# Mixture-of-experts stage: experts in 32 token places, four side by side in column quarters of the array, unrounded, weights in 8 KB runs

## The chip, the cores and the metric

One core of a Trainium2 chip runs the whole program. The metric is the device time of one execution in microseconds; the kernel before takes 2503.92 us, median of 3 runs (2502.22 to 2505.46).

## What is computed

The program is two blocks one behind the other on 256 tokens of width 1024, all in float32. The first has two layers of feed-forward, four kinds of attention and feed-forward again; the second has a gated delta rule, an RWKV-7 scan, their merge and a mixture of experts. Only the last concerns the change. Cut to it, the reference is:

```python
def hier_moe(h, router_grp, router_grp_b, router_exp, router_exp_b, w_gate, w_up, w_down):
    t = h.reshape(-1, h.shape[-1])                       # 256 tokens x 1024
    grp_p = softmax(t @ router_grp + router_grp_b)       # 4 groups
    p_grp, g_sel = lax.top_k(grp_p, 1)                   # one group to a token
    exp_logits = (t @ router_exp + router_exp_b).reshape(-1, 4, 8)
    in_grp = take_along_axis(exp_logits, g_sel)          # 8 experts of that group
    top_logit, top_idx = lax.top_k(in_grp, 2)            # two experts to a token
    w_top = softmax(top_logit) * p_grp
    combine = one_hot(group) * one_hot(expert) * w_top   # 256 x 4 x 8
    for grp in range(4):                                 # expert: 1024 -> 2 x 256 -> 1024
        hid = silu(t @ w_gate[grp]) * (t @ w_up[grp])
        out = out + (hid * combine[:, grp]) @ w_down[grp]

# in second_block, at its end
h_lat = h_lat + m_lat[2] * y_lat
h_lat = h_lat + m_lat[5] * hier_moe(modulate(rmsnorm(h_lat, norm_ffn_g), m_lat[3], m_lat[4]), ...)
return rmsnorm(h_lat, final_norm_g)
```

There are 32 experts, each with three matrices of 1 MB (gate and up 1024 x 256, down 256 x 1024), 100.7 MB in all.

## The kernel before

Everything is written out by hand for five engines, with semaphores that `did` and `at` number by name. Activations stand with the model's width on the partitions (`XT`, 8 tiles of 128 x 256 tokens).

**Weights.** All weights come over one queue, SP's, in the order of the list `jobs`. `load_ring` (L408, its DMA is L416) puts job j into slot j mod 3 of the ring `RB` (3 slots of 2 MB) as soon as the job three before it has been used up. `fill_e` (L334) fills a slot with an expert's gate and up matrices; a partition gets eight rows of each, every one a run of 1 KB. `fill_d` (L341) takes the down matrices of two experts, in runs of 4 KB.

**Products.** `mm` (L283, the matmul itself is L284) is one product. A float32 product leaves two records in the trace. `mm3` and, in the experts, the same thing written out, does a product in three rounded ones: ACT rounds half a slot into `gwh` (`Stream.high`, L440), DVE takes the rest into `gwl` (`Stream.low`, L449), activations are split likewise (`gxh`, `gxl`, `ghh`, `ghl`), and PE multiplies high by low, low by high and high by high. A slot is free when DVE has done its second half (`("low", "g", n)`).

**Around the experts.** `merge` (L3062) ends the second block's mixers: PE does four gate tiles (`gate1_pe`), the small product `glo`, turns, eight `merge` tiles and eight `out2` tiles, and between the `out2` tiles `Route.pe` does the router's products and turns the tokens. `places_dve` (L3362) then finds each token's group (`sel`, marked `grouped`), its place in the group by a product with a triangle (`ranks` in `places_pe`, L3320) and a 0/1 matrix `CHOSEN` of 128 tokens x 4 groups x 128 places. Then `known` says whether every group has at most 128 tokens; if so `gathered` (L3489) runs, else `dense` (L3622), over all tokens. `places_pe` gathers the tokens of all four groups at once by products with `CHOSEN` (`xm`), ACT scales them (L3352) and rounds them (L3355), DVE takes the rest (L3374).

**The experts.** `gathered` goes through 32 experts: 24 products of 128 places by 512 columns for gate and up, silu on ACT (L3571), times the token's weight on DVE (L3595), two turns (L3529), rounding, and 12 products of 512 columns down into the group's sums. Per group the sums are kept (L3582, L3609), and at the end products with the turned `CHOSEN` spread them over the tokens, and the last norm and its turns (`Finish`, L3749) run between them, up to the four stores (L3809).

Of the kernel before, what the change touches and what calls it, by code (L numbers as in the profile page):

```python
# [38 lines left out]
def constants():  # L39
# [21 lines left out]
    for k in range(6):  # L61
# [13 lines left out]
    pe_once="lam cum ab ab_parts route ranks cw glo wide_c spread shifted", eg="dg", ed="dd", columns="merge mgate out2 conv shift z",  # L75
    rw_in="w_in ic_in cums bon_in k_in", gdn_in="re_gate cumg wide_g kk kb_t",
    act_once="lam_exp sine f_log g_log beta group_exp expert_exp spread_root lnx_root o_root sil w2 low_act xd_high",
# [4 lines left out]
             "renorm_sq lnx_square a2 logits group_in expert_in combined rank known chosen cw_out cb_t xd_low rt_bias rt_w rstd_x grouped",  # L82
# [141 lines left out]
def program(nc, A, out, known):  # L224
    stack = ExitStack()
    with stack:
# [74 lines left out]
        jobs, job_no = [], {}  # L301

        def job(key, fill, free):
            job_no[key] = len(jobs)
            jobs.append((fill, free))
# [89 lines left out]
        pairs = [(("e", 0), ("e", 1))]  # L395
        pairs += [(("e", e), ("e", e + 1), ("d", e - 2)) for e in range(2, 32, 2)] + [(("d", 30),)]
        PAIRS = [x for step in pairs for x in step]
        first_expert = len(jobs)

        def slot_of(*key):  # L400
            return RB[:, job_no[key] % NSLOT, :]

        def landed(*key):
            return at(f"ring{job_no[key] % NSLOT}", job_no[key])

        sent = [0]

        def load_ring(upto_job):  # L408
            while sent[0] < upto_job:
                j = sent[0]  # L410
                if j >= NSLOT:
                    SP.wait_ge(*at(*jobs[j - NSLOT][1]))
                for i, (dst, src) in enumerate(jobs[j][0](RB[:, j % NSLOT, :])):
                    if i and one_by_one_from <= j < one_by_one_to:
                        SP.wait_ge(*at(f"ring{j % NSLOT}", j, i - 1))
                    nc.sync.dma_start(dst, src).then_inc(*did(f"ring{j % NSLOT}", j, i, by=16))  # L416
                did(f"ring{j % NSLOT}", j, by=0)
# [3468 lines left out]
```

## Time and profile before

| what | us |
|---|---|
| median of 3 runs | 2503.92 |
| span of the profiled execution | 2506.8 |
| PE busy in it | 2421.1 |
| DVE busy | 1408.6 |
| ACT busy | 1193.3 |

The profiled execution is 2.9 us above the median. Times below are counted from its start. The page's second part cuts the span into 40 slices of 62.7 us; the expert stage lies in the last five. PE is busy to 97% over the span, DMA moves 158 GB/s in the mean and over 360 GB/s in three of the last slices, so the mean hides that stage.

### The profile page before, as it was taken

What the parts mean: (1) busy time and instruction counts of PE and PEld (TensorE: products, weight loads), DVE (VectorE), ACT (ScalarE), POOL (GpSimd) and SP (SyncE); (2) the same over time, 40 slices, a digit from 0 to 9 for tenths busy, and PEclk for the clock granted to TensorE, in tenths of its full rate; (3) what the DMA queues carried; (4) which work ended last, traced back from release to release, by engine and by line L of the source; (5) the groups of instructions that cost most, each with busy time, mean ns of one, the idle gap of its engine ahead of it and who ended that gap; (6) DMA issues with size and microseconds to landing.
All of it is one profiled execution on the core that took longest, in us unless ns stands there. A gap on an engine that the chain in (4) does not pass through costs nothing.

```text
span 2506.8 us, 52399 instructions
## 1 busy us (share of the span) xinstructions
PE 2421.1 (97%) x23215; PEld 2091.8 (83%) x23215; DVE 1408.6 (56%) x2208; ACT 1193.3 (48%) x1725; POOL 296.2 (12%) x417
## 2 busy tenths in 40 slices
PE   7999999999999999999999999899999888999998
PEld 7999888799999998878899995686477777878887
DVE  5655544366646655543666567454434454378886
ACT  5434465444344444474454346431255342277775
POOL 0100000031101100000301000462133222000000
PEclk9999999999999999999999999999999989999999
DMA  8754522266656755422457522201201111479995
GB/s 262 243 205 152 205 92 92 105 202 216 223 183 202 236 185 179 146 97 106 143 193 236 213 77 101 70 3 40 68 35 37 33 42 46 131 246 365 368 364 181
DMA packets 269445, 396.15 MB, mean 158 GB/s; under 512 B 9624, under 2 KB 173133, under 8 KB 269085
## 3 DMA queue, kind: packets, MB, share of 16 engines
q1 hardware_dynamic: 267481, 389.32, 45.6%
q8 instruction: 185, 3.03, 0.5%
q0 software_dynamic: 1120, 2.17, 0.3%
q10 hardware_dynamic: 612, 1.24, 0.1%
q14 instruction: 47, 0.39, 0.0%
HBM read 391.66 MB, written 1.05 MB: 157 GB/s over the span
## 4 chain that ended last, share of the span: by engine, by line
PE 82%; DVE 6%; DMA 5%; ACT 3%; issue 2%; SPq 1%; POOL 0%; ACTq 0%; DVEq 0%
PE ps L284 81%; DMA RB<-in_moe_w_up 5%; DVE gwl L449 2%; ACT gwh L440 1%; SPq L521 1%; PE ps L1151 0%; SPq L416 0%; DVE wl L449 0%; DVE AR L659 0%; ACT wh L440 0%; ACT AR L2903 0%; DVE AR L1972 0%; PE ps L543 0%; ACT AR L2895 0%; ACT AT L1205 0%
## 5 line engine op out<-in xcount | busy, mean ns | idle before, releaser
L449 DVE TENSOR_TENSOR wl<-RB,wh 128x2048 fp32r<-128x2048 f32 (+5 forms) x189 | 412.2, 2185 | 281.1 <-ACT wh L440 280.6
L284 PE MATMUL ps<-H,RB 128*128 128x256 f32 (+2 forms) x1728 | 451.7, 420 | 2.8 <-ACT AR L2874 1.3
L440 ACT ACTIVATE wh<-RB 128x2048 fp32r<-128x2048 f32 (+5 forms) x189 | 342.2, 1814 | 227.4 <-PE ps L284 200.0
L284 PEld LDWEIGHTS ps<-H,RB 128*128 128x128 f32 (+1 forms) x1728 | 320.2, 189 | 113.7 <-issue 75.6
L284 PE MATMUL ps<-xhf,wl 128*128 128x256 f32 x1408 | 402.4, 286 | 2.4 <-DVE xlf L688 2.4
L284 PE MATMUL ps<-xlf,wh 128*128 128x256 f32 x1408 | 398.9, 283 | 0.0
L284 PE MATMUL ps<-xhf,wh 128*128 128x256 f32 x1408 | 398.8, 283 | 0.0
L284 PE MATMUL ps<-AR 64*64 64x64 f32 (+3 forms) x8296 | 264.6, 236 | 39.9 <-issue 24.7
L284 PEld LDWEIGHTS ps<-AR 64*64 64x64 f32 (+2 forms) x8296 | 231.4, 142 | 79.1 <-issue 64.2
L284 PEld LDWEIGHTS ps<-xhf,wl 128*128 128x128 f32 x1408 | 270.6, 192 | 13.2 <-issue 9.4
L284 PEld LDWEIGHTS ps<-xlf,wh 128*128 128x128 f32 x1408 | 270.8, 192 | 0.1
L284 PEld LDWEIGHTS ps<-xhf,wh 128*128 128x128 f32 x1408 | 270.6, 192 | 0.0
L449 DVE TENSOR_TENSOR gwl<-RB,gwh 128x2048 fp32r<-128x2048 f32 x96 | 217.2, 2289 | 37.2 <-ACT gwh L440 35.8
L440 ACT ACTIVATE gwh<-RB 128x2048 fp32r<-128x2048 f32 x96 | 183.0, 1925 | 44.1 <-DMA RB<-in_moe_w_up 30.8
L284 PE MATMUL ps<-hh,wl 128*128 128x256 f32 x704 | 199.2, 283 | 0.0
L284 PE MATMUL ps<-hl,wh 128*128 128x256 f32 x704 | 199.2, 283 | 0.0
L284 PE MATMUL ps<-hh,wh 128*128 128x256 f32 x704 | 199.2, 283 | 0.0
L793 ACT ACTIVATE H<-H 128x256 f32<-128x256 f32 x88 | 36.8, 419 | 296.0 <-DVE H L829 296.0
L284 PEld LDWEIGHTS ps<-hh,wl 128*128 128x128 f32 x704 | 135.2, 192 | 0.0
L284 PEld LDWEIGHTS ps<-hl,wh 128*128 128x128 f32 x704 | 135.2, 192 | 0.0
L284 PEld LDWEIGHTS ps<-hh,wh 128*128 128x128 f32 x704 | 135.2, 192 | 0.0
L1472 POOL TENSOR_TENSOR H<-H 128x256 f32<-128x256 f32 x48 | 47.6, 1026 | 680.5 <-DVE H L1443 680.3
(445 smaller groups left out, 4108.1 us busy)
## 6 DMA issues: line engine op xcount, KB each, us to landing
RB<-in_ffn_w_gu SPq DMA_DIRECT2D x88, 1024.0 KB, 7.7
RB<-in_w_in SPq DMA_DIRECT2D x23, 2048.0 KB, 7.8
RB<-in_ffn_w_down SPq DMA_DIRECT2D x16, 2048.0 KB, 7.8
RB<-in_w_gate SPq DMA_DIRECT2D x16, 2048.0 KB, 8.9
RB<-in_moe_w_gate SPq DMA_DIRECT2D x32, 1024.0 KB, 7.6
RB<-in_moe_w_up SPq DMA_DIRECT2D x32, 1024.0 KB, 10.2
RB<-in_moe_w_down SPq DMA_DIRECT2D x32, 1024.0 KB, 8.2
RB<-in_ada_w SPq DMA_DIRECT2D x12, 2048.0 KB, 9.9
```

Source lines behind the costliest of these rows:

```text
L284: return M.matmul(o, lhsT, rhs, start=start, stop=stop, skip_group_check=True)
L440: S.activation(self.pair(h)[0], of(slot_of(*key)), ACT.Copy).then_inc(*did("high", *mark))
L449: V.tensor_tensor(lo, of(slot_of(*key)), hi.bitcast(F32), ALU.subtract).then_inc(*did("low", *mark))
L521: nc.sync.dma_start(dst, src).then_inc(*did("late", by=16))
L793: S.activation(sil[:, n % 4, 0, :], sil[:, n % 4, 0, :], ACT.Silu).then_inc(*did("silu", f, n))
L1472: P.tensor_tensor(HB[:, c, :], HB[:, c, :], tmp[:, (8 * i + c) % 4, :], ALU.add).then_inc(*did("merged", l, br, c))
```

## The change

- **Loads.** `moe_jobs` lists, for each of eight steps of four experts, four gate-and-up jobs and two down jobs of two experts. Both fills give a partition one contiguous run of 8 KB per MB: row p·8+k of a matrix goes to partition p for gate and up, row p·2+h for down. Beside the three ring slots there are six more (`EX0` to `EX5`), in memory that the splits and the scan's buffers had; each opens at a mark in `opened`. Nine expert jobs are queued before the router has decided, and the second `out2` load comes behind the first three.
- **Order of the width.** Since a partition now holds rows p·8+k, tokens are gathered in that order (`UT` written strided), and the scale and shift vectors are brought into it once (`OWN`: five small DVE instructions and 8 + 1 small products in `merge`, one more copy, one product and a sum on DVE).
- **Places.** A rank is counted for each of 32 experts instead of each of 4 groups; `chosen` makes 32 places for each expert. The experts of a token must be known before the ranks, so that chain on DVE comes first. `known` asks for at most 32 tokens per expert. If an expert has more, `dense` runs, which is unrounded too.
- **Products.** Nothing is split or rounded. One step multiplies four experts, each by its own 32 places: stationary 128 x 32, moving 128 x 512, output in 32 of the 128 PSUM partitions. Per step these are 16 products for `gather`, 32 for `up`, 16 for `down` and 4 for `spread`, which adds straight into four banks of sums by token. `rows_pe` puts the residual into these banks first, `Y` is multiplied by the last gate as it leaves PSUM, and the last norm works on rows, without turns.

```diff
         def fill_e(e):
             def f(slot):
-                v = slot.rearrange("p (k g n) -> p k g n", k=KD, g=2)
-                return [(v[:, :, s, :], rows(A[n][0, e // 8, e % 8]))
+                v = slot.rearrange("p (s n) -> p s n", s=2)
+                return [(v[:, s, :], A[n][0, e // 8, e % 8].rearrange("(p k) n -> p (k n)", k=KD))
                         for s, n in ((0, "moe_w_gate_2"), (1, "moe_w_up_2"))]
             return f
 
-        def fill_d(e):
+        def fill_d(n, x):
             def f(slot):
-                v = slot.rearrange("p (e k n) -> p e k n", e=2, k=2)
-                return [(v[:, u], rows(A["moe_w_down_2"][0, e // 8, e % 8 + u])) for u in range(2)]
+                e = 4 * (n % 2) + 2 * x
+                return [(slot.rearrange("p (e n) -> p e n", e=2), A["moe_w_down_2"][0, n // 2, e:e + 2].rearrange(
+                    "e (p h) n -> p e (h n)", h=2))]
             return f
...
+        out2_last = jobs.pop()
+
+        slots = [RB[:, i, :] for i in range(NSLOT)] + [sb(f"EX{i}", STAGE + c, [4096]) for i, c in enumerate(
+            (13568, 17664, 21760, 9472, 4736))] + [sb("EX5", O_H, [4096])]
+        opened = {3: [("rw_out", 7, 1)], 4: [("rw_out", 7, 1)], 5: [("rw_out", 7, 1)], 6: [("turned", "ya", 1)],
+                  7: [("summed", 7)], 8: [("mgate", 1, 7), ("glo", 1)]}
+        expert_slots = (3, 4, 5, 8, 6, ring_jobs[0] % NSLOT, (ring_jobs[0] + 1) % NSLOT, (ring_jobs[0] + 2) % NSLOT, 7)
 
...
+        sent, holder = [0], {}
 
         def load_ring(upto_job):
             while sent[0] < upto_job:
                 j = sent[0]
-                if j >= NSLOT:
-                    SP.wait_ge(*at(*jobs[j - NSLOT][1]))
-                for i, (dst, src) in enumerate(jobs[j][0](RB[:, j % NSLOT, :])):
+                fill, free, slot = jobs[j]
+                if slot in holder:
+                    SP.wait_ge(*at(*jobs[holder[slot]][1]))
+                else:
+                    for mark in opened.get(slot, ()):
+                        SP.wait_ge(*at(*mark))
+                holder[slot] = j
+                for i, (dst, src) in enumerate(fill(slots[slot])):
...
+                PE.wait_ge(*at("own_in"))
+                ps = bank(("own_rows",), ("own_16",))
+                for k in range(KD):
+                    ins = mm(ps[0:16, 16 * k:16 * k + 16], ident.rearrange("p (q k) -> p k q", k=KD)[:, k, :], OWN_IN,
+                             True, True)
+                ins.then_inc(*did("own_rows"))
...
+                ps = bank(("own",), ("own_out",))
+                PE.wait_ge(*at("own_16"))
+                mm(ps[:, 0:128], RST[0:16, 128:256], RST[0:16, 0:128], True, True).then_inc(*did("own"))
...
+                V.tensor_copy(OWN_IN[:, 0:8], SCL[:, 2, :])
+                V.tensor_copy(OWN_IN[:, 8:16], MOD[:, 24:32, 0])
+                V.tensor_copy(RST[0:16, 128:256].rearrange("p (c q) -> p c q", c=8),
+                              ident[0:16, 0:16].unsqueeze(1).broadcast_to([16, 8, 16]))
+                V.tensor_reduce(IN_16, ident.rearrange("p (c j) -> p c j", c=8), AXX, ALU.add)
+                V.tensor_reduce(IN_32, ident.rearrange("p (c j) -> p c j", c=4), AXX, ALU.add).then_inc(*did("own_in"))
...
+            ring_jobs[0] = ring_at_experts
+            of_experts = [(kind, n, x) for n in range(8) for kind, x in
+                          (("e", 0), ("e", 1), ("e", 2), ("e", 3), ("d", 0), ("d", 1))]
+            for i, (kind, n, x) in enumerate(of_experts):
+                if i == 3:
+                    job_no[("out2", 1)] = len(jobs)
+                    jobs.append(out2_last)
+                slot = expert_slots[i % len(expert_slots)]
                 if kind == "e":
+                    job(("e", 4 * n + x), fill_e(4 * n + x), ("eg", n) if branch == "g" else ("dg", 4 * n + x), slot)
                 else:
+                    job(("d", n, x), fill_d(n, x),
+                        ("dd", n, x) if branch == "d" else ("y", n, 1), slot)
...
-                self.ws_g = Split("g", Stream(self.wh, self.wl), halves)
...
+            def rows_pe(self):
+
+                for c in (0, 4):
+                    for t in LAT:
+                        ps = bank(("acc", t, c // 4), among=(4, 5, 6, 7))
+                        for j in range(4):
+                            ins = mm(ps[:, 128 * j:128 * j + 128], XT[:, c + j, 128 * t:128 * t + 128], ident, j == 0,
+                                     False)
+                ins.then_inc(*did("acc"))
...
+                one = self.px.rearrange("p t g e -> p t (g e)")
+                PE.wait_ge(*at("picked"))
+                mm(ps[:, 64:96], ones, one[:, 0], True, False)
+                mm(ps[:, 64:96], ones, one[:, 1], False, True)
+                mm(ps[:, 0:32], cst(C_PAIR), one[:, 0], True, True)
+                mm(ps[:, 32:64], ones, one[:, 0], True, False)
+                mm(ps[:, 32:64], cst(C_PAIR), one[:, 1], False, True).then_inc(*did("ranks"))
...
+                def chosen(t, n0, n1):
+                    e = 4 * (n1 - n0)
+                    return V.tensor_tensor(
+                        self.CHOSEN[:, t, n0:n1].rearrange("p n (e s) -> p (n e) s", e=4),
+                        CST[:, C_NUM + 1:C_NUM + 33].unsqueeze(1).broadcast_to([128, e, 32]),
+                        rank[:, t, 4 * n0:4 * n1].unsqueeze(2).broadcast_to([128, e, 32]), ALU.is_equal)
...
+                def gather(n):
+                    for t in LAT:
+                        PE.wait_ge(*at("chosen", t, min(n, 2)))
+                    for half in range(2):
+                        ps = bank(("xm", n, half), ("xm_out", n, 4 * half + 3), among=work)
+                        for k in range(4 * half, 4 * half + 4):
+                            for t in LAT:
+                                if n == 0 and k == 0:
+                                    PE.wait_ge(*at("u_rows", t, 4))
+                                ins = mm(ps[:, 128 * (k % 4):128 * (k % 4) + 128], UT[:, t, k, :], CHOSEN[:, t, n], t == 0,
+                                         t == 1)
+                        ins.then_inc(*did("xm", n, half))
+
+                def up(n):
+                    ps = bank(("up", n), ("h_scaled", n), among=work)
+                    for k in range(KD):
+                        PE.wait_ge(*at("xm_out", n, k))
+                        for c in range(4):
+                            PE.wait_ge(*landed("e", 4 * n + c))
+                            ins = mm(ps[32 * c:32 * c + 32, :].rearrange("p (s n) -> p s n", s=2),
+                                     XG[n % 2][:, k, 32 * c:32 * c + 32], up_of(4 * n + c)[:, :, k, :], k == 0, k == KD - 1)
+                    ins.then_inc(*did("eg", n))
+
+                def back(n):
+                    turn(("turned", "back", n), [("back", n)], [CHOSEN[:, t, n] for t in LAT], among=work)
+
+                def turned(n):
+                    PE.wait_ge(*at("h_scaled", n))
+                    turn(("turned", "h", n), [("h_out", n)], [S1[n % 2].rearrange("p (q h) -> p h q", h=2)[:, h, :] for h in range(2)], among=work)
+
+                def down(n):
+                    ps = [bank(("y", n, o), ("y_out", n, o), among=work) for o in range(2)]
+                    PE.wait_ge(*at("h_out", n))
+                    for x in range(2):
+                        PE.wait_ge(*landed("d", n, x))
+                    w = [slot_of("d", n, x).rearrange("p (e h n) -> p e h n", e=2, h=2) for x in range(2)]
+                    for o in range(2):
+                        for half in range(2):
+                            for c in range(4):
+                                ins = mm(ps[o][32 * c:32 * c + 32, :], HT[n % 2][:, half, 32 * c:32 * c + 32],
+                                         w[c // 2][:, c % 2, half, 512 * o:512 * o + 512], half == 0, half == 1)
+                        ins.then_inc(*did("y", n, o))
+
+                def spread(n):
+                    PE.wait_ge(*at("back", n))
+                    for t in LAT:
+                        for o in range(2):
+                            PE.wait_ge(*at("y_out", n, o))
+                            ins = mm(accs[2 * t + o], BACK[n % 2][:, 128 * t:128 * t + 128], Y[:, 512 * o:512 * o + 512],
+                                     False, n == 7)
+                            if n == 7:
+                                ins.then_inc(*did("moe_sum", t, o))
+                    if n < 7:
+                        ins.then_inc(*did("spread", n))
...
-                        ps = bank(("up", "g", e), ("h_scaled", e), among=work)
-                        for half in range(2):
-                            hi, lo = ws.weights(ups[e] + half)
-                            for i in range(4):
-                                k = 4 * half + i
-                                PE.wait_ge(*at("xm_low", k))
-                                a, c = xh[:, k, 128 * g:128 * g + 128], xl[:, k, 128 * g:128 * g + 128]
-                                mm(ps[:, :], c, hi[:, i, :], k == 0, False)
-                                mm(ps[:, :], a, lo[:, i, :], False, False)
-                                ins = mm(ps[:, :], a, hi[:, i, :], False, k == KD - 1)
-                            ins.then_inc(*did("eg", e, half))
-                    elif what == "turn":
-                        ps = bank(("turned", "h", e), ("h_low", e), among=work)
...
+                for n in range(8):
+                    if n:
+                        up(n)
+                        if n < 7:
+                            gather(n + 1)
+                    back(n)
+                    turned(n)
+                    down(n)
+                    spread(n)
...
+                def places(n):
+                    for k in range(KD):
+                        AC.wait_ge(*at("xm", n, k // 4))
+                        if n > 1 and k == 0:
+                            AC.wait_ge(*at("eg", n - 2))
+                        S.activation(XG[n % 2][:, k, :], ps_of("xm", n, k // 4)[:, 128 * (k % 4):128 * (k % 4) + 128],
+                                     ACT.Identity, bias=PV[:, k, 1:2], scale=PV[:, k, 0:1]).then_inc(*did("xm_out", n, k))
...
+                for t in LAT:
+                    for o in range(2):
+                        AC.wait_ge(*at("moe_sum", t, o))
+                        S.activation(SQ[o], accs[2 * t + o], ACT.Square, accum_out=SS[:, t, o:o + 1]).then_inc(
+                            *did("squared", "end", t, o))
+                    AC.wait_ge(*at("sums", t))
+                    S.activation(SS[:, t, 2:3], SS[:, t, 2:3], ACT.Sqrt, bias=EPS[:, 0:1], scale=1.0 / DM).then_inc(
+                        *did("root", "end", t))
+                AC.wait_ge(*at("rstd", "end", 1))
...
+                for n in range(8):
+                    DV.wait_ge(*at("h_silu", n))
+                    V.scalar_tensor_tensor(out=S1[n % 2], in0=S1[n % 2], scalar=CW[:, n:n + 1], in1=ps_of("up", n)[:, 256:512],
+                                           op0=ALU.mult, op1=ALU.mult).then_inc(*did("h_scaled", n))
+                    DV.wait_ge(*at("turned", "h", n))
+                    if n > 1:
+                        DV.wait_ge(*at("y", n - 2, 1))
+                    V.tensor_copy(HT[n % 2].rearrange("p a n -> p (a n)"), ps_of("turned", "h", n)[:, 0:T]).then_inc(
+                        *did("h_out", n))
+                    for o in range(2):
+                        DV.wait_ge(*at("y", n, o))
+                        DV.wait_ge(*at("m5", o))
+                        if n:
+                            DV.wait_ge(*at("spread", n - 1))
+                        V.tensor_tensor(Y[:, 512 * o:512 * o + 512], ps_of("y", n, o), M5[:, 512 * o:512 * o + 512],
+                                        ALU.mult).then_inc(*did("y_out", n, o))
```

## Rows read from the trace of the kernel before

**Rows 1.** The page: span, then DMA share (tenths) and GB/s in 40 slices.
```profile
span 2506.8 us, 52399 instructions
...
DMA  8754522266656755422457522201201111479995
GB/s 262 243 205 152 205 92 92 105 202 216 223 183 202 236 185 179 146 97 106 143 193 236 213 77 101 70 3 40 68 35 37 33 42 46 131 246 365 368 364 181
```

**Rows 2.** Stretches (start:end, length, busy us and count by engine, clock, DMA share, GB/s).
```profile
2148.00:2184.40 36.40, 36.35 (x208) 32.62 (x206) 9.16 (x13) 6.94 (x11) 0.00 (x0) 1.00 0.40 120
2184.40:2190.60 6.20, 2.14 (x11) 2.06 (x11) 3.73 (x24) 4.17 (x7) 0.00 (x0) 0.66 0.94 310
2190.60:2210.00 19.40, 19.40 (x57) 9.83 (x57) 9.78 (x30) 12.43 (x18) 0.00 (x0) 0.84 0.34 109
2210.00:2485.00 275.00, 273.45 (x1224) 222.29 (x1222) 237.50 (x166) 203.46 (x169) 0.00 (x0) 1.00 0.98 336
2485.00:2507.00 22.00, 13.04 (x106) 12.46 (x106) 6.51 (x13) 9.67 (x22) 0.00 (x0) 0.85 0.15 51
```

**Rows 3.** SP: its waits (us, times, longest); its DMA issues in time.
```profile
SPq L416 <- DVE gwl L449: 218.0, 44, 24.8
...
2217.36 0.88 SPq L416 DMA_DIRECT2D RB<-in_moe_w_down  x2
```

**Rows 4.** Groups of instructions 2185 to 2502: busy us, mean ns, idle before.
```profile
L284 PE MATMUL ps<-gwh,gxl 128*128 128x512 f32 x256 | 101.8, 397 | 0.1
L284 PE MATMUL ps<-AR 128*128 128x512 f32 x32 | 17.0, 697 | 2.2 <-DVE SM L3416 2.2
L3529 PE MATMUL ps<-CST,AR 128*128 128x128 f32 x64 | 12.1, 270 | 0.0
L3609 DVE TENSOR_TENSOR gxl<-ps,gxh 128x512 fp32r<-128x512 f32 x8 | 5.1, 683 | 4.5 <-ACT gxh L3582 4.5
```

**Rows 5.** PE in order of time, 2112 to 2169: start, us, instruction, count.
```profile
2112.14 1.97 PE L284 MATMUL ps<-SM 128*128 128x36 f32 x16
...
2127.93 1.95 PE L284 MATMUL ps<-H,AR 128*64 128x256 f32 x16
...
2164.88 3.70 PE L284 MATMUL ps<-AR,RB 128*128 128x256 f32 x16
```

**Rows 6.** Weight loads beside them, 2126 to 2134: ns min/median/max, first and last start.
```profile
L284 PEld LDWEIGHTS ps<-H,AR x16: 132/137/137, 2127.9 to 2129.3; 128*64 128x64 f32 x16
```

**Rows 7.** Stretches: down in runs of 4 KB twice, gate and up of 1 KB.
```profile
2220.00:2224.00 4.00, 4.00 (x21) 3.25 (x20) 4.00 (x5) 2.87 (x4) 0.00 (x0) 1.00 1.03 417
...
2222.00:2223.00 1.00, 1.00 (x6) 0.83 (x5) 1.00 (x2) 1.00 (x1) 0.00 (x0) 1.00 1.05 434
...
2234.00:2236.00 2.00, 2.00 (x10) 1.67 (x9) 1.76 (x4) 1.50 (x2) 0.00 (x0) 1.00 1.10 350
```

**Rows 8.** Stretches: the scan, then two short ones around the router.
```profile
2050.00:2100.00 50.00, 40.89 (x1543) 37.66 (x1543) 24.91 (x61) 17.88 (x43) 19.10 (x32) 0.93 0.04 7
...
2186.00:2188.00 2.00, 1.77 (x9) 1.77 (x10) 0.43 (x3) 1.98 (x4) 0.00 (x0) 0.61 1.07 364
...
2196.00:2198.00 2.00, 2.00 (x6) 0.79 (x5) 0.58 (x1) 0.66 (x1) 0.00 (x0) 0.83 1.10 355
```

**Rows 9.** DVE in order of time: before the merge, and around the router.
```profile
2129.14 1.48 DVE L3170 TENSOR_TENSOR AR<-AR,ps 128x512 f32<-128x512 f32 x2 [2.99 <-PE ps L284]
...
2186.21 0.22 DVE L3399 TENSOR_TENSOR AR<-AR 128x64 f32<-128x64 f32 x1
...
2190.53 0.26 DVE L3417 TENSOR_REDUCE AR<-AR 128x16 f32<-128x64 f32 x1
...
2192.45 0.17 DVE L3438 TENSOR_TENSOR AR<-AR 128x16 f32<-128x16 f32 x1
```

**Rows 10.** The end in order of time: ACT's root, DVE's scaling.
```profile
2499.39 0.26 ACT L3786 ACTIVATE SM<-ps,SM 128x2 f32<-128x2 f32 x1 [0.70 <-PE ps L284]
...
2499.88 1.41 DVE L3801 TENSOR_SCALAR AR<-ps,SM 128x512 f32<-128x512 f32 x2
```

More of the change, by code:

```diff
@@ L74 @@
 SHARED = {name: sem for sem, names in dict(
-    pe_once="lam cum ab ab_parts route ranks cw glo wide_c spread shifted", eg="dg", ed="dd", columns="merge mgate out2 conv shift z",
+    pe_once="lam cum ab ab_parts route ranks cw glo wide_c spread shifted own_rows own acc m5_rows", eg="dg", ed="dd", columns="merge mgate out2 conv shift z",
     rw_in="w_in ic_in cums bon_in k_in", gdn_in="re_gate cumg wide_g kk kb_t",
-    act_once="lam_exp sine f_log g_log beta group_exp expert_exp spread_root lnx_root o_root sil w2 low_act xd_high",
+    act_once="lam_exp sine f_log g_log beta group_exp expert_exp spread_root end_root xd_out lnx_root o_root sil w2 low_act",
     rows="k_rows v_rows rv_rows o_rows u_rows back ob b_rows k_rows_r", h_high="d_high yk_high", h_silu="d_silu",
@@ L298, in everyone, with job @@
                     x.wait_ge(*at(*mark))
-        jobs, job_no = [], {}
-        def job(key, fill, free):
+        jobs, job_no, ring_jobs = [], {}, [0]
+        def job(key, fill, free, slot=None):
             job_no[key] = len(jobs)
-            jobs.append((fill, free))
+            if slot is None:
+                slot = ring_jobs[0] % NSLOT
+                ring_jobs[0] += 1
+            jobs.append((fill, free, slot))
         def fill_gu(w, c):
@@ L3121, in tensor @@
                 route.pe(KD - 1)
+                route.rows_pe()
             def scalar():
@@ L3459, in places_dve @@
                     *did("combined"))
-                for k in range(3, KD):
-                    low_x(k)
-                    if k == 4:
-                        self.ws_g.low(3)
         def experts(route):
@@ L3472, in experts @@
             fits = nc.values_load(route.FLAG[0:1, 0:1], min_val=0, max_val=1)
-            here = ([dict(x.seen) for x in (PE, DV, AC, PO, SP)], dict(counts.n), dict(bank_at), list(bank_free), sent[0])
+            here = ([dict(x.seen) for x in (PE, DV, AC, PO, SP)], dict(counts.n), dict(bank_at), list(bank_free), sent[0],
+                    dict(holder))
             with nc.If(fits > 0):
                 load_ring(len(jobs))
-                gathered(area, route)
+                gathered(route)
             for x, seen in zip((PE, DV, AC, PO, SP), here[0]):
@@ new lines, in scalar @@
+                AC.wait_ge(*at("owned"))
+                for k in range(KD):
+                    AC.wait_ge(*at("xd", k))
+                    S.activation(XM[:, k, :], ps_of("xd", k)[:, 0:T], ACT.Identity, bias=PV[:, k, 1:2],
+                                 scale=PV[:, k, 0:1]).then_inc(*did("xd_out", k))
+                for j, (n, c, i) in enumerate(order):
+                    AC.wait_ge(*at("dg", 4 * n + c))
+                    if j > 1:
+                        AC.wait_ge(*at("c_scaled", *order[j - 2]))
+                    S.activation(S1[:, j % 2, :], ps_of("up", "d", n, c, i)[:, 0:T], ACT.Silu).then_inc(
+                        *did("d_silu", n, c, i))
```

499 lines of the change are left out of this document (185 added, 314 removed).

## The prediction, made before the kernel ran

> **What bounds the kernel now.** I read the page's slices first, then busy time by stretches, then SP's waits, then groups of instructions in the expert stage. Over the whole span DMA moves little, but from slice 36 to 39 it is busy to nine tenths at 365 to 368 GB/s [rows 1]. The change touches only what comes after 2110, so the last 400 us are all that counts. There the stages are [rows 2]: `out2` with the router's products to 2184.4, PE full; the choice of places to 2190.6, PE busy 2.1 of 6.2 us; gathering to 2210, PE full but at a clock of 0.84; the experts to 2485, PE busy 273.5 of 275.0 us; the end, 22 us. PE bounds the expert stage. Its 36 products to an expert start every 0.23 us (1152 products and 64 turns in 275 us). That DMA looks full too is no second bound: SP waited 218.0 us, 44 times, for DVE to free a slot [rows 3], so three slots hold the loads to PE's pace.
>
> **What the change takes away.** All of those 275 us of rounded products, with ACT's and DVE's splits beside them, and the 19.4 us of gathering. What replaces them is bounded by the slower of two streams, PE's and DMA's.
>
> **PE's new price.** An unrounded product of 128 x 256 costs 3.70/8 = 0.46 us with its neighbours' overlap, or 0.43 by the pace of full rows [rows 5]; of 512 columns 0.85 us, two records (the 16 `xm` products left 32 records with a mean of 0.70 us at a mixed clock [rows 4]). If four side by side run at once, `up` costs 8 x 0.85 = 6.8 us a step and `down` 4 x 0.85 = 3.4. Do they? The nearest row is `glo`: eight products of 256 columns with 64 stationary columns, in the two column halves in turn, took 1.95 us in 16 records [rows 5]; one behind the other they would be 8 x 0.43 = 3.4. Two at once is shown at full gain; four at once is not. Bounds: four at once, or two at once (`up` 13.6, `down` 6.8). I take four, since the gain of two was whole.
>
> The Trainium skill ("TensorE: Matmul & The Clock Gate", Part 3, What overlaps and what doesn't) speaks against it: weight loads overlap running products only where the row group differs, and column quarters share all rows. The `glo` weight loads took 137 ns each and their 16 records still came every 107 ns [rows 6]; so the trace doesn't agree with that rule for halves. By it, 96 loads a step would stand bare, about 96 x 0.11 = 10.6 us, which gives 30 us a step instead of 19.
>
> The rest of a step: `gather` 16 products of 128 columns, no cheaper than the 128x36 ones at 1.97/8 = 0.246 [rows 5], so 3.9 us; four turns at 0.135 each, 0.5 (two records of 0.27 overlap [rows 4]); `spread` 4 x 0.85 = 3.4; waits of PE for the copy of the turned tile 0.5 and for the second half of `Y` 0.7, as 128x512 takes DVE 0.68 [rows 4]. `gather` of the next step hides silu and weighting (under 1 us). Sum: 6.8 + 3.4 + 3.9 + 0.5 + 3.4 + 1.2 = 19.2 us a step. ACT (eight scalings, silu, one copy) and DVE (about 2.3 us) lie under it.
>
> **DMA's new price.** A step needs 6 x 2.097 = 12.6 MB. Runs of 1 KB flow at 350 GB/s, runs of 4 KB at 417 over 4 us and 434 in the best single microsecond [rows 7]. No row shows 8 KB. Bounds: 350 (no gain) to 434; I take 417, the nearest run length. That is 30.2 us a step, more than PE's 19.2, so **DMA becomes the bound** and PE idles about 11 us in 30.
>
> Two rules of the Trainium skill differ here ("DMA: Bandwidth & Descriptors"). Where 436 GB/s comes from says that the HBM side, about 358 GB/s to a core, binds; the trace's 417 and 434 disagree. Measured gives 425 for one core with a large transfer, an estimate by which the stream below is 192.5 us instead of 196.1.
>
> **The sum, on the clock of the profiled execution.**
>
> 1. To `route`. On PE `own_rows` (8 narrow products) and `own` come onto the path, 1 to 2.2 us by 0.12 to 0.246 each; I take 1.5. The DVE instructions (about 1 us at first, 0.7 later) are hidden: DVE ends early and waits 2.99 us for `glo` [rows 9]. If the chain were 2 us longer, PE would wait. The early loads go behind the first `out2` load and ahead of the second, which is needed only at 2166; 6.3 MB in front of it are 15 us from 2112. SP passes all its waits in order. Result 2184.4 + 1.5 = 2185.9.
> 2. The places. `grouped` stands as before. The chain from the reduction to the last sum, 2190.5 to 2192.6, now comes before the ranks [rows 9]: +2.2 us. Eight `chosen` comparisons of 1.66 us before become two, about 0.6: -1.1. `rows_pe` (16 products, 3.9 us) runs in PE's idle time. First gather at 2190.6 + 1.5 + 1.1, about 2193.5 with 0.3 of waiting.
> 3. `gather` and `up` of step 0. The clock fell to its lower level of 1.2 GHz in 2186 to 2188, after PE had idled, and rose again in 2196 to 2198 [rows 8], 6 us after work began. I let it do the same: 7.0 us of gathering, then 6.8. End 2207.3. Both at full clock would give 2204, both at half 2214.
> 4. Then slots open again. By now nine of 48 expert jobs are in (the ninth is sent when `out2` ends, 4.2 MB with the eighth, 10 us). Left: 39 x 2.097 = 81.8 MB, at 417 GB/s 196.1 us. End of loads 2403.4. A stall would come if `y` of step 0 were later than 20 us after `up`; I count `cw` 3.9, gather 3.9, `m5_rows` 2.0, turns 0.5, wait 0.5, down 3.4 = 14.2. From there the slack grows.
> 5. Behind the last load: `down` 3.4, `Y` 0.8, `spread` 3.4, and 2.7 because PE has been idle and starts at the low clock; square, root and scaling 2.0; stores 5.5, as from the last scaling's end at 2501.3 to 2506.8 [rows 10]. Together 17.8.
>
> End 2403.4 + 17.8 = 2421.2, that is 85.6 below 2506.8. The profiled execution lies 2.9 above the median, so 2503.9 - 85.6 = **2418.3 us**.
>
> **The rivals.**
>
> - *The transfers gain nothing from longer runs.* For: the mean was 366 over whole slices [rows 1], and no row has 8 KB. Against: 417 at 4 KB. At 366 the stream takes 223.5 us: 2446. At 350 it is 234: 2456.
> - *Only two quarters run at once*, or weight loads stand bare. A step is 19.2 + 6.8 + 3.4 = 29.4 us, about equal to DMA's. The first `up` ends at 2214.1; then 8 steps, 235.2, less one `up` and one `gather`, 17.5, with 6 for `cw` and `m5_rows` and 7.5 behind the last `spread`: 2445.3, as a median 2442.
>
> The page's rule on weight loads gives 30 us a step, 5 more in all.
> - *Slower: the quarters run one behind the other.* `up` 27.3 and `down` 13.7 make a step 50.0 us; eight steps 400, from 2200.5, less one `gather` 3.9, with 6 and 7.5: 2610, as a median 2607, 103 slower. It decides from a step of (2506.8 - 2200.5 - 9.6)/8 = 37.1 us, that is below 1.5 quarters at once. Against it: the halves in `glo`.
> - *No gain: the clock.* DMA-bound PE idles 11 us in each 30, and the clock falls after idling [rows 8]. If it stayed at 1.2 GHz for the whole stage, a step would be 18 x 2 + 1.2 = 37.2, eight 298; from 2200.5, less 7.8 for a `gather`, with 12 and 7.5: 2510, as a median 2507, just about no change, and slower with any other loss. Against it: in the scan PE is idle 9 of 50 us and works in 64x64 tiles, at a clock of 0.93 [rows 8], and a PE that slow would not idle at all. One slow start in each step costs 3 us of the 11 to spare, nothing.
> - *It doesn't do what it says*: an expert with over 32 tokens sends everything down the dense branch, 32 x 16 x 0.85 + 32 x 16 x 0.43 = 655 us, about 2870. The reference's own routing of these inputs gives the fullest expert 27 tokens, so this has almost no chance.
>
> **How the numbers follow.** Forecast (DMA-bound, 400 to 434 GB/s, 2410 to 2430) 0.60; transfers without gain or partly 0.15; two at once or bare loads, and other PE costs that end in 2430 to 2460, 0.15; one behind the other 0.05; the clock 0.04; dense 0.01. The range reaches from 434 GB/s with `up` at full clock (2407) down a little for the end stage, 2403, to the cases at 2445 and 2456: 2455. A measurement of this kernel can tell about 0.2%, 5 us, from no change. Faster 0.89: the first three cases are 0.90, less 0.01 for what no row shows, which goes to no change. Slower 0.08: 0.05, half of the clock's 0.04 and 0.01. Within 0.2% 0.03.
>
> **What would show it.** In the profile after: DMA at 400 or more GB/s from about 2207 to 2403 with a share near 1, PE idle some 10 us in 30 and waiting for `in_moe_w_gate` or `in_moe_w_down`; `up` records every 107 ns at full clock; the first `up` ended by 2207; the last load 18 us before the end. Wrong would be: PE busy without gaps, records every 213 ns, SP waiting for PE, or a lasting clock of 0.5.

## The result and the profile after

The changed kernel takes **2414.74 us**, median of 4 runs (2412.0 to 2415.13), the kernel before 2503.07 beside it (2501.75 to 2505.46): a ratio of 0.9646 (95% interval 0.9632 to 0.966), 88 us less. The forecast was 2418.3. Its profiled execution took 2412.8 us.

The page of the changed kernel, where [rows 1] stood: span and instructions, busy time by engine, then clock, DMA share and GB/s in slices that are now 60.3 us long.

```profile
span 2412.8 us, 51780 instructions
...
PE 2293.6 (95%) x23049; PEld 1925.2 (80%) x23049; DVE 1178.6 (49%) x2070; ACT 1003.7 (42%) x1613; POOL 297.5 (12%) x417
...
PEclk9999999999999999999999999999999999999998
DMA  8754533255655754442346752220111101177997
GB/s 266 244 201 166 175 128 105 88 202 184 213 210 165 255 202 174 165 138 85 110 171 200 241 192 74 105 72 4 41 70 37 39 20 57 34 287 293 420 420 322
```

DVE and ACT are little used in the last slices, and DMA is at 420 GB/s where it was at 366. Executions differ by some us before the stage that was changed: `out2` and the router's products end at 2180.4 here and at 2184.4 before, although this change only adds to what comes ahead of them, and in another execution of the changed kernel (`e10_same` below) they end at 2190.4. I therefore also count every run from the end of the router's last product (the last `128x2` product that `Route.pe` issues) to the end of the span, and call that **the rest**. It was 322.4 us before (2506.8 - 2184.4) and is 232.4 now: 90.0 less.

Stretches of the changed kernel, columns as in [rows 2]: the choice of places; the first `gather`; the first `up`; the stage; behind it. The last two lines show where the loads really stop.

```profile
2180.40:2188.70 8.30, 4.95 (x42) 4.84 (x42) 5.31 (x33) 5.73 (x8) 0.00 (x0) 1.00 1.02 425
2188.70:2192.50 3.80, 3.79 (x36) 3.68 (x37) 2.46 (x9) 1.51 (x4) 0.00 (x0) 1.00 0.67 262
2192.50:2199.50 7.00, 7.00 (x66) 1.97 (x65) 0.00 (x0) 2.79 (x5) 0.00 (x0) 1.00 0.01 3
2199.50:2395.80 196.30, 156.96 (x1030) 67.96 (x1027) 16.41 (x30) 26.67 (x72) 0.00 (x0) 0.91 1.01 416
2395.80:2413.00 17.20, 9.48 (x54) 2.92 (x45) 6.52 (x15) 6.12 (x15) 0.00 (x0) 0.90 0.21 78
...
2396.00:2397.00 1.00, 1.00 (x6) 0.11 (x1) 0.00 (x0) 0.00 (x0) 0.00 (x0) 1.00 0.43 180
2397.00:2398.00 1.00, 0.47 (x3) 0.20 (x2) 0.44 (x1) 0.84 (x3) 0.00 (x0) 1.00 0.00 0
```

The fourth line is the stage: DMA full for 196.3 us, PE at work in 157.0 of them. The loads then thin out: the last packet of a weight ends at 2397.2, and the last load counts as landed at 2397.6. The third line is a gap: all nine slots are full, nothing can be loaded until the first `up` frees four.

One stretch of the chain that ended last, in order of time (start, us, what).

```profile
2336.92 20.89 DMA EX<-in_moe_w_up
...
2357.86 8.97 PE ps L284 x58
...
2366.84 0.33 SPq L429
...
2367.21 20.47 DMA EX<-in_moe_w_up
...
2387.72 9.39 PE ps L284 x58
```

PE's 9 us stand in the chain, although DMA doesn't stop in them. The profile draws it so: `up` frees a slot, SP sends a load into it, and that load lands 20 us later, behind those already queued. The waits from 2200 on, PE's and SP's (us, times, longest), can be read either way too: each stream waits for the other.

```profile
PE ps L284 <- DMA EX<-in_moe_w_up: 25.7, 8, 4.2
...
PE ps L284 <- DMA RB<-in_moe_w_up: 5.8, 3, 3.9
```
```profile
SPq L429 <- PE ps L284: 67.8, 8, 10.6
```

SP waited 67.8 us for slots and DMA was full all the same, since the loads sent before had not landed yet. The chain alone would give PE a third of the stage; the rate in the windows shows that the queue never ran dry. So the first question was which of the two it is.

### The profile page after: what moved, and what is told of

Read it like the earlier page. It is cut to its first block, busy times and chain, and to the rows that moved or that the text cites. A ratio compares the mean times of both kernels' runs of the same rounds, so it can differ in the third digit from the quotient of the medians.

```text
span 2412.8 us, 51780 instructions
## 1 busy us (share of the span) xinstructions
PE 2293.6 (95%) x23049; PEld 1925.2 (80%) x23049; DVE 1178.6 (49%) x2070; ACT 1003.7 (42%) x1613; POOL 297.5 (12%) x417
## 4 chain that ended last, share of the span: by engine, by line
PE 86%; DMA 5%; DVE 3%; ACT 2%; issue 2%; SPq 1%; POOL 0%; ACTq 0%; DVEq 0%
PE ps L284 85%; DMA EX<-in_moe_w_up 3%; DMA RB<-in_moe_w_up 1%; SPq L535 1%; PE ps L1165 0%; DVE wl L462 0%; DVE AR L673 0%; SPq L429 0%; ACT wh L453 0%; DVE AR L1986 0%; PE ps L557 0%; ACT AT L1219 0%; ACT AR L2917 0%; ACT AR L2909 0%; DMA VR<-in_diff_gain 0%
## 5 line engine op out<-in xcount | busy, mean ns | idle before, releaser
L284 PE MATMUL ps<-AR 64*64 64x64 f32 (+6 forms) x8536 | 275.8, 232 | 37.8 <-issue 24.6
L284 PEld LDWEIGHTS ps<-AR 64*64 64x64 f32 (+3 forms) x8536 | 250.5, 141 | 72.9 <-issue 61.5
L284 PE MATMUL ps<-EX,AR 128*32 128x512 f32 x528 | 104.0, 659 | 31.7 <-DMA EX<-in_moe_w_up 25.7
L1486 POOL TENSOR_TENSOR H<-H 128x256 f32<-128x256 f32 x48 | 47.7, 1029 | 680.5 <-DVE H L1457 680.3
L880 POOL TENSOR_TENSOR H<-H 128x256 f32<-128x256 f32 x88 | 65.4, 743 | 474.0 <-ACT H L807 474.0
```

The lines of the kernel that those rows point to most:

```text
L284: return M.matmul(o, lhsT, rhs, start=start, stop=stop, skip_group_check=True)
L880: P.tensor_tensor(sil[:, n % 4, 0, :], sil[:, n % 4, 0, :], sil[:, n % 4, 1, :], ALU.mult).then_inc(*did("hidden", f, n))
L1486: P.tensor_tensor(HB[:, c, :], HB[:, c, :], tmp[:, (8 * i + c) % 4, :], ALU.add).then_inc(*did("merged", l, br, c))
```

## The experiments

**Which stream bounds the stage.** One step of `up` in the changed kernel costs 7 us of PE. The kernel `e5_up_twice` does it twice:

```diff
-                    for k in range(KD):
+                    for again in range(2):
+                        for k in range(KD):
...
-                                     ..., k == 0, k == KD - 1)
+                                         ..., k == 0, k == KD - 1)
```

> The changed kernel with every step's 32 `up` products done twice (the second pass starts the sums anew, so the result is the same). Theory (transfers bound): the first pass delays the release of the first slots by 7 us and the last one the end by 7; the six between vanish in PE's idle time (19.2 + 7 = 26 under 30). 2415 + 14 = 2429. Rival (PE bounds the stage): 8 x 7 = 56 more, 2471.

Measured: 2431.41 us median of 2 (ratio to before 0.9707, 0.9679 to 0.9735); the rest 247.0 us, 14.6 more. Of 56 us of added products 41 vanish. Its stretch from 2250 to 2350:

```profile
2250.00:2350.00 100.00, 92.28 (x728) 36.68 (x728) 7.56 (x13) 11.01 (x30) 0.00 (x0) 1.00 1.01 420
```

PE is busy to 92% and DMA still moves 420 GB/s. The clock is at its upper level of 2.4 GHz throughout; PE idles 7.7 of 100 us.

The other way round, `e4_pe_floor` takes the bytes away:

```diff
-                return [(v[:, s, :], A[n][0, e // 8, e % 8].rearrange("(p k) n -> p (k n)", k=KD))
+                m = 2048 if e < 8 else 256
+                return [(v[:, s, 0:m], A[n][0, e // 8, e % 8].rearrange("(p k) n -> p (k n)", k=KD)[:, 0:m])
```

and the same for down from step 2 on.

> The changed kernel where from the third step on only an eighth of every expert run is loaded (the rest of the slot keeps older weights, so the numbers are not the reference's). Theory: the step falls from 30 us to PE's own price of 19.2 to 20 us, so from step 2 on 6 x 10.5 us less: about 2350, and the clock stays at its upper level. Rival (PE costs more than I counted, and both bound together): a fall of under 30 us.

Measured: 2361.6 us (2361.5 and 2361.7; ratio 0.9432, 0.9407 to 0.9457); the rest 177.2, 55.2 less. PE no longer waits for any weights. In order of time (start, us, products), the `spread` of three steps:

```profile
2235.43 3.72 PE L284 MATMUL ps<-CST 128*128 128x512 f32 x8
...
2255.14 3.72 PE L284 MATMUL ps<-CST 128*128 128x512 f32 x8
...
2274.84 3.72 PE L284 MATMUL ps<-CST 128*128 128x512 f32 x8
```

A step is 19.7 us of PE; the prediction had put it at 19.2. I had expected 63 us less and got 55, because I had taken the difference of 10.5 us for six steps. In the changed kernel only five steps wait for weights: its first three `spread`s start at 2213.4, 2233.1 and 2254.3, nearly at PE's pace, and the last one at 2402.7. From the third to the last are 148.4 us there and 95.1 here, 53.3 less; the first steps give 1.5 more. Both experiments agree with transfers as the bound and not with PE.

**Does every early byte count?** `e8_late_loads` sends only three expert jobs ahead:

```diff
-        load_ring(first_expert + len(expert_slots) + 1)
+        load_ring(first_expert + 4)
```

> The changed kernel with only three expert jobs and the second `out2` load sent ahead; the other six wait until the branch is known, about 2188. Theory (the end is the sum of what is left to load): 45 jobs from 2188 at 4.99 us instead of 39 from 2199.6, 19 us more, 2434, and no gap in the transfers at 2190 to 2200. Rival (PE bounds the stage): 5 us at most, since three to four jobs are enough to start the first step.

Measured: 2437.9 us median of 2 (0.9733, 0.9704 to 0.9761); the rest 256.3, 23.9 more, against 19 expected. SP issues the first of the late loads at 2190.5, 11.4 us behind the router's last product, and the last of the 45 lands at 2421.0, 230.5 us later. That is 5.1 us a job, as in the changed kernel (198.0 us for 39, from 2199.6 to 2397.6); 14.4 us follow. Six jobs more are 31 us; 8 of them come back, because the loads needn't wait for the first `up` (11.4 us behind the router instead of 19.2). The theory stands, the rival of 5 us doesn't.

**Run length.** `e1_runs1k` gives gate and up their old runs:

```diff
-                return [(v[:, s, :], A[n][0, e // 8, e % 8].rearrange("(p k) n -> p (k n)", k=KD))
+                return [(v[:, s, :].rearrange("p (k n) -> p k n", k=KD), rows(A[n][0, e // 8, e % 8]))
```

> The changed kernel with the gate and up weights again in runs of 1 KB (down stays in 8 KB; the width's order then doesn't match, so the experts' numbers are not those of the reference, but every instruction and the routing are the same). Theory (transfers bound the expert stage): 26 of the 39 jobs behind the first `up` run at about 350 instead of 421 GB/s, 6.0 instead of 5.0 us each, so 26 us more, 2441. Rival (PE bounds it, and the gain came from fewer and packed products): no change, 2415. Rival (what counts is only that the loads are ahead): no change.

Measured: 2442.91 us median of 4 (0.9757, 0.9735 to 0.9779), 28 more than the changed kernel; the rest 261.6, 29.2 more. 26 us are the stream (223.4 us from the end of the first `up` to the last packet, against 197.7); the first `up` ended 3.1 us later, as the clock had fallen (below). `e2_runs4k` gives everything runs of 4 KB:

```diff
-                return [(v[:, s, :], A[n][0, e // 8, e % 8].rearrange("(p k) n -> p (k n)", k=KD))
+                return [(v[:, s, :].rearrange("p (a m) -> p a m", a=2),
+                         A[n][0, e // 8, e % 8].rearrange("(a p j) n -> p a (j n)", a=2, j=4))
```

and down alike.

> The changed kernel with all expert weights in runs of 4 KB instead of 8 KB (numbers not the reference's, as the width's order doesn't match; the work is the same). Theory: 4 KB runs reach 417, so 195 to 197 us for the stream, 0 to 2 us more than with 8 KB, 2415 to 2417. Rival (8 KB itself is what brought the rate from 350 to 420): half the gain lost, about 12 us more.

Measured: 2417.3 us median of 4 (0.9655, 0.9635 to 0.9676); the rest 237.8, 5.4 more. 30 us of each, first 1 KB, then 4 KB, then the changed kernel with 8 KB:

```profile
2320.00:2350.00 30.00, 20.18 (x128) 8.45 (x124) 2.29 (x4) 3.67 (x10) 0.00 (x0) 0.84 1.08 362
```
```profile
2300.00:2330.00 30.00, 21.54 (x140) 8.75 (x132) 2.29 (x4) 3.66 (x10) 0.00 (x0) 0.90 1.03 409
```
```profile
2300.00:2330.00 30.00, 23.43 (x144) 9.19 (x140) 2.29 (x4) 3.67 (x10) 0.00 (x0) 0.90 1.02 422
```

The first line is a mean over gate and up in 1 KB and down in 8 KB. From 4 KB to 8 KB the rate rises by 3%, 5.7 us on 81.8 MB. I had expected 0 to 2; 409 here is a mean of 30 us, the 417 of [rows 7] one of 4 us. In the rest, 1.5 us come from a first `up` that ended later, and the tail was shorter by about as much. Nearly the whole gain of the layout was there at 4 KB.

**What bounded the kernel before.** `e3_before8k` is the kernel before with the 8 KB runs alone:

```diff
-                v = slot.rearrange("p (k g n) -> p k g n", k=KD, g=2)
-                return [(v[:, :, s, :], rows(A[n][0, e // 8, e % 8]))
+                v = slot.rearrange("p (s n) -> p s n", s=2)
+                return [(v[:, s, :], A[n][0, e // 8, e % 8].rearrange("(p k) n -> p (k n)", k=KD))
```

and down alike.

> The kernel before, its order and three slots kept, only with its expert weights in runs of 8 KB (numbers not the reference's, as the width's order doesn't match). Theory (PE bounded the expert stage before): within 3 us of 2503, with DMA less busy in slices 36 to 39 and the same 365 GB/s. Rival (loads bounded it together with PE): the stage shrinks with the rate, up to 25 us faster.

Measured: 2500.38 us median of 10 against 2503.27 (ratio 0.9991, 0.9978 to 1.0004): no change that can be told. Its expert stage:

```profile
2205.00:2480.00 275.00, 273.99 (x1248) 225.39 (x1247) 242.49 (x169) 205.99 (x175) 0.00 (x0) 1.00 0.86 336
```

Beside [rows 2], a stretch of the same length: the same 336 GB/s, but at a DMA share of 0.86 instead of 0.98. The longer runs made the loads cheaper and nobody waited for them. So the parts don't add up: the change without the long runs of gate and up brings 60 us (2443), the long runs alone at most 6 by their interval (2500), and both together 88. No run has the new products with three slots, so what the six further slots bring apart from the early loads (`e8_late_loads`) isn't shown.

**Side by side or in turn.** `e6_in_turn` changes only the order of products in `up` and `down`, one expert's after the other's:

```diff
-                    for k in range(KD):
-                        PE.wait_ge(*at("xm_out", n, k))
-                        for c in range(4):
+                    for c in range(4):
+                        for k in range(KD):
+                            PE.wait_ge(*at("xm_out", n, k))
...
-                        for half in range(2):
-                            for c in range(4):
+                        for c in range(4):
+                            for half in range(2):
```

> The changed kernel with only the order of the products changed: in `up` and `down` all products of one expert's column quarter, then the next (the result is the same). Theory (quarters only overlap when neighbours in the order differ in their quarter): `up` 27.3 and `down` 13.7 us, a step of 50 us, PE-bound, about 2600: the slower rival of the prediction, made real. Rival (PE looks ahead far enough, or a quarter product is cheap by itself): 2415.

Measured: 2487.29 us median of 3 (0.9924, 0.9902 to 0.9947). The direction is the theory's and the size isn't: 73 us more, not 185. The first `up` and two `spread`s in order of time:

```profile
2194.17 22.59 PE L284 MATMUL ps<-EX,AR 128*32 128x512 f32 x64
...
2232.25 3.72 PE L284 MATMUL ps<-CST 128*128 128x512 f32 x8
...
2267.52 3.72 PE L284 MATMUL ps<-CST 128*128 128x512 f32 x8
```

A step is 35.3 us. `up` takes 22.6 instead of 27.3, and `down` has lost nothing: 3.68 for its 32 records, where it took 3.64 side by side. Where only two products of one quarter follow each other, those of the next quarter still ran at the same time. So PE starts products of another quarter ahead of their turn, over a short distance. In the second `up` the products with weights in `RB` all come first in the program, those with weights in `EX` all behind them. The first `EX` record still starts before the last three `RB` records:

```profile
2246.26 0.62 PE L284 MATMUL ps<-EX,AR 128*32 128x512 f32 x1
2246.69 0.59 PE L284 MATMUL ps<-RB,AR 128*32 128x512 f32 x1
2246.72 0.59 PE L284 MATMUL ps<-EX,AR 128*32 128x512 f32 x1
2247.12 0.59 PE L284 MATMUL ps<-RB,AR 128*32 128x512 f32 x1
2247.15 0.59 PE L284 MATMUL ps<-EX,AR 128*32 128x512 f32 x1
2247.55 0.59 PE L284 MATMUL ps<-RB,AR 128*32 128x512 f32 x1
```

By an estimate from the two totals, 27.3 less 22.6 over three changes of quarter, each change saves 1.6 us, about four records of 0.43.

**The clock at the router.** In the changed kernel it stayed at 1.00 through the choice of places, where it had fallen before [rows 8]. `e7_no_rows` takes the products of `rows_pe` out, so that its output lacks the residual:

```diff
-                        for j in range(4):
-                            ins = mm(ps[:, 128 * j:128 * j + 128], XT[:, c + j, 128 * t:128 * t + 128], ident, j == 0,
-                                     False)
+                ins = mm(ps[:, 0:2], XT[:, 7, 128:256], ident[:, 0:2], True, True)
...
-                                     False, n == 7)
+                                     n == 0, n == 7)
```

> The changed kernel without the 16 products of `rows_pe` that put the residual into the sums (so the output lacks it); one product of two columns stands in for the mark. Theory (they kept PE busy through the choice of places, and that is why the clock never fell there): the clock falls to 0.5 at about 2186, the first `gather` and part of `up` run slowly, the first `up` ends 3 to 6 us later counted from `out2`, total 2417 to 2420. Rival (the clock stayed up for another reason): 2415 or up to 1 us less.

Measured: 2418.35 us (2414.73 and 2421.97; ratio 0.9655, 0.9614 to 0.9695), too wide to tell; the rest is 235.7, 3.2 more. Stretches of it:

```profile
2186.00:2188.00 2.00, 0.00 (x0) 0.00 (x0) 1.79 (x14) 2.00 (x4) 0.00 (x0) 0.50 1.06 446
...
2196.00:2198.00 2.00, 2.00 (x11) 2.00 (x11) 0.09 (x1) 0.55 (x2) 0.00 (x0) 0.50 0.07 27
...
2198.00:2200.00 2.00, 2.00 (x14) 1.93 (x12) 0.00 (x0) 0.95 (x3) 0.00 (x0) 0.69 0.00 0
```

PE idled 4.5 us, the clock fell to 0.50, its lower level, and the first `up` ended 22.6 us after the router instead of 19.2. But it is no rule: in `e1_runs1k`, `e2_runs4k`, `e6_in_turn` and `e8_late_loads`, which have `rows_pe` and issue the same products there, the clock fell too in the profiled execution (the products of `rows_pe` took 5.5 to 6.8 us instead of 3.9), and the first `up` of `e1_runs1k`, `e2_runs4k` and `e8_late_loads` ended 22.3, 20.7 and 29.4 us after the router (the last one waited for weights as well). In the other five with `rows_pe` it stayed up. Without it there are three executions, this one, the kernel before and `e3_before8k`, and it fell in all three; with four of nine against three of three, whether the filler makes the fall rarer isn't shown.

**A try to beat it.** `e9_warm` puts products into PE's waits, so that the last `up` finds the clock up:

```diff
+                    if n > 1:
+                        for _ in range(7):
+                            mm(ps, ident, Y[:, 0:512], True, True)
```

> The changed kernel with seven idle products (128x512, overwritten by the first `up` product) ahead of each `up` from step 2 on, where PE waits for the weights (the result is the same). Theory (the transfers bound the stage; the clock counts only behind the last gate and up weights): steps 2 to 6 gain nothing; the last `up` takes 7.1 instead of 9.4 us, so `down` starts 2.0 to 2.5 us earlier, 2412 to 2413. Rival (slow products in every step cost time): 2 us in each of 6 steps, 12 less, 2403. Rival (the added products get in the way of the weights' arrival): 0 to 5 us more.

> The changed kernel as it is, beside the one with idle products on the same chip, as its measure: 2415, within 2 us.

Measured beside each other: 2416.47 us (2413.72 to 2422.81, ratio to before 0.9656, 0.9637 to 0.9674) and 2420.63 (2415.79 to 2424.29, 0.9664, 0.9647 to 0.968): the intervals overlap. The rest is 231.6 against 232.1 us, so 0.5 of the 2 to 2.5 expected. Stretches of `e9_warm` around its last `up`:

```profile
2384.00:2388.00 4.00, 4.00 (x14) 1.29 (x13) 0.00 (x0) 0.00 (x0) 0.00 (x0) 1.00 1.02 422
2388.00:2390.00 2.00, 0.41 (x3) 0.00 (x0) 0.00 (x0) 0.00 (x0) 0.00 (x0) 1.00 1.01 418
...
2394.00:2396.00 2.00, 2.00 (x16) 0.61 (x12) 0.00 (x0) 0.00 (x0) 0.00 (x0) 0.51 1.01 418
```

PE's last records ended 3.1 us before the weights came, the seven products some 4 us before, and the clock still fell, only later: the last `up` took 8.8 us from there instead of 9.2 in `e10_same`. It isn't a version to keep. The same kernel measured 2414.7 in one set of runs and 2420.6 in the other, with the rest equal to 0.3 us: the difference lies ahead of the experts.

## Why the prediction was right, point by point

- **PE bounded the stage before, through the slots.** Right: `e3_before8k` moves it by 0.9991 with cheaper loads.
- **PE's new price, 19.2 us a step.** Measured 19.7. Four quarters do run at once: 64 records of the first `up` in 7.07 us, one each 110 ns; one behind the other they would take 27.3.

```profile
2192.47 7.07 PE L284 MATMUL ps<-EX,AR 128*32 128x512 f32 x64
```

  The weight loads of that `up` in order of time (start, us, count, idle time before), and all of them (ns minimum, median, maximum; first and last start):

```profile
2192.93 0.13 PEld L284 LDWEIGHTS ps<-EX,AR 128*32 128x32 f32 x4 [0.30 <-issue]
2193.36 0.13 PEld L284 LDWEIGHTS ps<-EX,AR 128*32 128x32 f32 x4 [0.30 <-issue]
```
```profile
L284 PEld LDWEIGHTS ps<-EX,AR x64: 106/110/110, 2192.5 to 2198.5; 128*32 128x32 f32 x64
```

  A quarter's weights take 110 ns, those of four quarters overlap to 0.13 us, and PE's weight port then idles 0.30 us until the next four. They add nothing, so the price of 30 us a step by the Trainium skill's rule ("TensorE: Matmul & The Clock Gate", Part 3, What overlaps and what doesn't: weight loads overlap only across row groups) isn't this chip's for column quarters.
- **DMA's rate, 417 of 350 to 434.** Measured 419 to 422 in stretches of 30 us. From the end of the first `up` to the landing of the last load the 39 jobs took 198.1 us; predicted 196.1. At 421 GB/s they would take 194.3; the rest passes before the first packet (2200.6) and in the last 2 us, where the rate falls. That 417 came so near is partly luck: it was the rate of 4 KB runs over 4 us, which over 30 us is 409, and the 8 KB runs were faster by about as much as start and end cost. The 358 of the Trainium skill ("DMA: Bandwidth & Descriptors", Where 436 GB/s comes from) is passed by 17%; the page's Measured section gives that figure for each of two cores that stream together and 425 for a lone one, as here, which is within 2%.
- **To `route`, +1.5.** From the start of the 128x36 products of [rows 5] (2112.1 before, 2107.0 now) to the router's last product 72.2 became 73.4: +1.2. `own_rows` cost 0.70 and `own` 0.48.
- **The places.** Predicted 81.4 us from that start to the first gather, measured 2188.7 - 2107.0 = 81.7. From the router's last product alone it is 8.3, predicted 7.6.
- **The first `gather` and `up`, 13.8.** Measured 10.8. This is the term that was off: I let the clock fall as before. In this execution it didn't; where it did, in `e7_no_rows`, the first `up` ended 3.4 us later.
- **The tail, 17.8.** Measured 15.2, and not the way that was forecast. I put `down` straight behind the last load, with `down`, `Y` and `spread` slow at first, 10.3 us. In fact the last gate and up weights came at 2387.7, the last `up`, at the low clock at first, ended at 2397.1, and silu, weighting, turn and copy came after it: `down` started at 2399.1, 1.5 us behind the last load (2397.6). By then the clock was up, and `down` and `spread` took 7.3; 6.4 follow them, where I had 7.5. The end waits for the last gate and up weights, not for the last down weights.
- **PE's idle time, 11 us in 30.** Too much: PE is idle 6.6 to 8.4 us in each 30, at a clock of 0.88 to 0.90. The low clock after each wait takes 2 to 3 us of it, as counted. The rest I put down to `up` beginning piece by piece, as each of four experts lands (from 2256 to 2260 PE is busy 3.0 us with only 9 records); no run separates it.
- **The sign "SP waiting for PE".** It was listed as a sign of being wrong, and it is there: 67.8 us in 8 waits. It isn't one, as DMA had enough queued to stay at 420 GB/s; the sign of a PE-bound stage would be SP waiting *and* a lower rate, as in `e6_in_turn`, where SP waits 212.7 us for PE and DMA moves 345 to 348 GB/s in the middle of the stage. The weights that PE's waits name are those of up, which are issued last of each pair of gate and up, and not gate or down as forecast. On the page before, the slices at 365, 368 and 364 GB/s are 37 to 39; slice 36 has 246.
- **Rivals.** No gain from longer runs: what `e1_runs1k` is, 2443, close to the 2446 worked out for 366 GB/s. One behind the other: `e6_in_turn` had its step priced at 50 us and took 35.3, still under the 37.1 from which the change would lose. The clock for the whole stage: never below 0.88 in any 30 us of the changed kernel.

From the router's last product on, the forecast had 2421.2 - 2185.9 = 235.3 us and the trace has 232.4, 2.9 less: the first `gather` and `up` 3.0 less and the tail 2.6 less, the places 0.7 more and the loads 2.0 more. So part of the agreement is errors that cancel. On the profile's clock the forecast of 2421.2 is 8.4 too high, 5.5 of it ahead of the router's last product, where executions of one kernel differ by up to 10 us. By medians the change was forecast at -85.6 us and measured at -88.3. The bound and its rate were right; that the medians agree to 3.6 us is closer than the 5.9 us by which the changed kernel's own medians differ.

## What to carry to other kernels

When a stage is split between two streams, price both before and after: here the quarters with the old 1 KB runs of gate and up gave 2443 us, the new runs without quarters 2500, and both together 2415, because the first part moves the bound to the stream that the second part speeds up. Small stationaries that share their rows should be issued in turns over the column quarters, four experts a round; but two products of one quarter in a row cost nothing. Once a stage is bound by its loads, three things beside their rate move its end: bytes loaded before it starts, the moment at which the first buffers come free, and what stands behind the last weights that a chain of work waits for.

## What was not expected of the hardware

- PE starts products of another column quarter ahead of older ones of the quarter before, over a short distance: `down` in turn costs 3.68 us against 3.64, `up` in turn 22.6 instead of 27.3.
- With many loads queued, issuing one holds SP for microseconds. Before, an issue took 0.37 to 2.05 us between 2200 and 2300; in the changed kernel's DMA issues in order of time (start, us):

```profile
2246.62 4.76 SPq L429 DMA_DIRECT2D RB<-in_moe_w_down  x1
2251.42 4.32 SPq L429 DMA_DIRECT2D RB<-in_moe_w_gate  x1
2255.79 2.14 SPq L429 DMA_DIRECT2D RB<-in_moe_w_up  x1
```

  It cost nothing here, since SP has nothing else to send. A small urgent load on that queue would presumably stand behind it; no run tried that.
- The same instructions around the router found the clock at 1.00 in some executions and at 0.50 in others, worth up to 3 us.
